# A fused two-block kernel on one Trainium2 core: the last unit of the gate z moves from the projection stage to the head of the delta stage

## The chip, the cores and the metric

The kernel runs on one core of a Trainium2 chip. The metric is the device time of one launch in microseconds (us). Everything below is in us unless a row says ns.

## What is computed

The reference runs a block of two layers (a mixer and a feed-forward part each) and then a second block. The change lies in the mixer of the first block, which runs once per layer, so twice in a launch. Cut to what matters here:

```python
p = h @ w_in                       # h: 512 tokens x 1024
(qkv, z, beta_r, a_r, hq, ...) = _split(p, IN_SIZES)
qkv = silu(_dwconv(qkv, dn_conv))  # q, k, v of 4 heads x 128; q and k are brought to unit norm
o_f = _gated_delta_rule(q, k, v, beta[0], g[0])
o_b = _flip(_gated_delta_rule(_flip(q), _flip(k), _flip(v), _flip(beta[1]), _flip(g[1])))
o_dn = o_f + o_b
o_dn = o_dn * rsqrt(mean(o_dn**2) + EPS) * dn_norm * silu(z)
```

z is 512 wide. It is made in four units of 128 rows, one for each head, and is needed only when the delta rule's output is gated, after the delta rule is done.

## The kernel before, in words

Everything is kept as 128-partition tiles of 512 columns (the tokens). A dense product of a weight tile and the input is made of three matmuls for each of eight k tiles, because weights and input are each split into a high part (rounded) and a low part (the rest): `product` (lines 142 to 148) writes high x high (L145), high x low (L146) and low x high (L147). One unit of 128 output rows is 24 matmuls of 512 columns. The queues of the five engines are written out by hand; each stage is one block, all engines leave a block together, and the engines meet by semaphores inside it.

The mixer's stages around the change:

- `qkv_stage` (line 332) makes 16 units: 12 for q, k and v and 4 for z (units 12 to 15). SP loads the raw weights of each unit into one of four buffers; ScalarE (ACT) rounds them (`high`, L379 to L383), GpSimd (POOL) or VectorE (DVE) makes the low part, TensorE (PE) multiplies (`dense`, L454 to L457). At the end of PE's queue stand unit 14, the transposes of the values (`turned_values`, L479 to L487) and then unit 15. At the end of ACT's queue stand the copies of the turned values (L440) and, in a loop over four, the SiLU of each z unit from its PSUM bank into Z (L441 to L443). The squares that the norms need lie in the buffer OHG during this stage.
- `delta_stage` (line 617) runs the delta rule in chunks of 128 tokens, in two directions (lanes 0 and 1, m counts the chunks). Its head, before the loop over m: PE makes the small gate sums (`gates_small`, L748, 16 columns each), the cumulated gates (`cumulated`, L758) and the products of keys with keys (`keys`, L766). DVE and ACT make decays from them (L1027, L925), DVE the masked scores (L1038), ACT scales them by beta (L939), POOL masks them for each level (`level_mask`, L676, tile LB). Then the triangular inverse is built level by level: `level_p` on PE (L786), a copy by ACT (`keep_p`, L952), `level_d` on PE (L794), a subtraction and a transpose by DVE (L1054, L1057). SP loads the next stage's first weights, 2 MB, at the start of this stage. The buffer OHG is free at first; the delta rule's R and VN lie in it from the first chunk's end on.
- `hgrn_proj_stage` (line 1153) makes the next products, and DVE multiplies the normed output of the delta stage by Z (L1327). ACT makes SiLUs there anyway (L1282).

The PSUM has eight banks; lane 0 of the delta stage has banks 0 to 3, lane 1 banks 4 to 7. Bank 2 of lane 0 is first written by `queries`, in turn m = 1 of the loop.

The lines that set the order at the seam are these (PE's queue at the end of `qkv_stage`, ACT's, and PE's head of `delta_stage`):

```python
                for h in range(4):
                    turned_values(h)
                dense(15)
...
                for j in range(4):
                    act.wait_ge(used, 13 + j)
                    act.activation(Z[:, j, :], PS[:, (12 + j) % 6, :], ACT.Silu).then_inc(S["z_done"], 1)
...
                for d in lanes:
                    keys(0, d)
                for m in range(CH + 1):
```

Of the kernel before, what the change touches and what calls it, by code (L numbers as in the profile page):

```python
# [14 lines left out]
P = 128  # L15
F32 = mybir.dt.float32
F32R = mybir.dt.float32r
# [313 lines left out]

def qkv_stage(nc, signals, PS, C, A, l, X, SS, XD, x_kept, pair, QKV, KTOK, VTOK, Z, BETA, G, SMALL, PAR, S1, S2, R, new):

# [13 lines left out]
    with signals.stage(*names) as sems:  # L347
# [12 lines left out]
        with nc.Block() as block:  # L360
# [17 lines left out]
            def _(act):  # L378
                def high(u):  # L379
                    act.wait_ge(loaded[u % N], 16 * (u // N + 1))  # L380
                    if u >= N:
                        act.wait_ge(used, u - N + 1)
                    act.copy(WHI[:, u % N], RAW[:, u % N]).then_inc(hi_s, 1)  # L383

# [53 lines left out]
                for h in range(4):  # L438
                    act.wait_ge(S["values_turned"], h + 1)
                    act.copy(tok(VTOK, h), PS[:, 6 + (h + 1) % 2, :].rearrange("p (c d) -> p c d", d=P)).then_inc(S["values_kept"], 1)  # L440
                for j in range(4):  # L441
                    act.wait_ge(used, 13 + j)
                    act.activation(Z[:, j, :], PS[:, (12 + j) % 6, :], ACT.Silu).then_inc(S["z_done"], 1)  # L443

            @block.tensor
            def _(pe):
# [78 lines left out]
                for h in range(4):  # L525
                    turned_values(h)
                dense(15)

# [77 lines left out]
            @block.gpsimd  # L606
            def _(pool):
                for u in range(N, T):
                    pool.wait_ge(hi_s, u + 1)
                    pool.tensor_tensor(WLO[:, u % N], RAW[:, u % N], WHI[:, u % N], ALU.subtract).then_inc(lo_pool, 1)  # L610

# [4 lines left out]

def delta_stage(nc, signals, PS, C, QKV, KTOK, VTOK, BETA, G, O, spare, parked, new, early):

# [11 lines left out]
    for d in lanes:  # L630
# [6 lines left out]
    kinds = ("small", "ngc", "ld", "mk", "gc", "m", "eg", "e", "kk", "at", "aq", "atb", "aqb", "lb", "tt0", "tc", "p", "pc", "dd", "t",  # L637
             "p6", "tcd", "d6", "ttf", "qk", "qkc", "qkm", "kg", "ks", "r", "vn", "vnc", "qg", "o", "oc", "oa", "kd", "st", "sd", "su")
    with signals.stage(*[f"delta_{n}{d}" for n in kinds for d in lanes]) as sems:
# [14 lines left out]
        with nc.Block() as block:  # L654
# [89 lines left out]
            def _(pe):  # L744
# [24 lines left out]
                def queries(m, d):  # L769
                    if m:  # L770
                        pe.wait_ge(S["oc" if m <= 2 else "oa"][d], m if m <= 2 else m - 2)
                    for h in H4:
                        last = pe.matmul(hb(d, 2, h), k_of(h, chunk(m, d)), q_of(h, chunk(m, d)), start=True, stop=True)
                    last.then_inc(S["qk"][d], 1)
# [92 lines left out]
                for d in lanes:  # L867
                    keys(0, d)
                for m in range(CH + 1):
                    j, levels, after = m - 1, m < CH, m + 1 < CH  # L870
# [47 lines left out]
            def _(act):  # L918
# [64 lines left out]
                for m in range(CH + 1):  # L983
                    j, levels, after = m - 1, m < CH, m + 1 < CH

                    def keep(n):
                        if levels:
                            for d in lanes:
                                keep_p(m, d, n)

                    keep(1)
                    if m:
                        for d in lanes:
                            keep_last(j, d)
                    keep(2)
                    if after:
# [156 lines left out]
def hgrn_proj_stage(nc, signals, PS, C, CR, l, A, SMALL, pair, O, Z, dn_norm, LF, KK, HI, HQ, HG, new, early):  # L1153
# [8 lines left out]
    with signals.stage("weights_hi", "weights_lo", "projected", "vector_steps", "scalar_steps", "logits_in", "reach_in", "tables_cast", "bound",  # L1162
# [3 lines left out]
        for g in range(5):  # L1166
            pnames += [f"unit{g}_0", f"unit{g}_1"] if g < 3 else [f"unit{g}_{m}" for m in range(4)]
        proj = Steps(proj_s, pnames)
        act_st = Steps(act_s, [f"{a}{g}_{c}" for g in range(2) for q in (0, 2) for a in ("e", "ln1", "lnb", "inv") for c in (q, q + 1)]
                       + [f"hi{c}" for c in range(4)] + [f"silu{g}_{m}" for g in (3, 4) for m in range(4)])  # L1170
        dve_st = Steps(dve_s, [n for g in range(2) for q in (0, 2) for n in [f"lbe{g}_{c}" for c in (q, q + 1)] + [f"{a}{g}_{c}" for c in (q, q + 1) for a in ("er", "kk", "lf")]]
# [11 lines left out]
        with nc.Block() as block:  # L1183
# [50 lines left out]
            def _(act):  # L1234
# [41 lines left out]
                for c in range(4):  # L1276
                    act_st.done(act.copy(HI[:, c, :], bank(2, c)), f"hi{c}")
                act.wait_ge(dve_st.sem, dve_st.place["lf1_3"])
                for g, dst in ((3, HQ), (4, HG)):
                    for m in range(4):  # L1280
# [6 lines left out]
            def _(dve):  # L1287
# [37 lines left out]
                for h in range(4):  # L1325
                    dve.wait_ge(norm_s, h + 1)
                    dve.tensor_tensor(O[:, h, :], O[:, h, :], Z[:, h, :], ALU.mult).then_inc(norm_s, 1)  # L1327
                for m in range(4):
# [1705 lines left out]
def mixer_layers(nc, signals, PS, C, A, X, XD, SS, PARS, SMALLS, new_in):  # L3034
    for l in range(A["w_in"].shape[0]):
        PAR, SMALL = PARS[:, 2 * l:2 * l + 2, :], SMALLS[:, l, :]
        w_in_l = A["w_in"][l].rearrange("(k p) n -> p k n", p=P)
        with ExitStack() as ffn, ExitStack() as mix:
            new = new_in(mix)
            pair = split_pair(new)  # L3040
            ODN, OHG = new("ODN", [P, 4, 512]), new("OHG", [P, 4, 512])
            with ExitStack() as zs:
                new_r = new_in(zs, "right")
# [3 lines left out]
                with ExitStack() as dn:  # L3047
# [5 lines left out]
                    BETA = new("BETA", [P, 4, 8])  # L3053
                    G = new("G", [P, 4, 8])
                    with ExitStack() as w:
                        R = hgrn_early.raw[:, :, :, :].rearrange("p s k n -> p (s k n)").rearrange("p (t n) -> p t n", n=512)
                        qkv_stage(nc, signals, PS, C, A, l, X, SS, XD, x_kept, pair, QKV, KTOK, VTOK, Z, BETA, G, SMALL, PAR[:, 0, :], OHG, ODN, R, new_in(w))
                    delta_stage(nc, signals, PS, C, QKV, KTOK, VTOK, BETA, G, ODN, OHG, X, new, hgrn_early)
                LF = new_in(mix)("LF", [P, 8, 512])
# [52 lines left out]
```

## Time and profile before

| | us |
|---|---|
| time, median of 3 runs | 2964.24 |
| lowest and highest | 2963.05, 2968.63 |
| the profiled execution's own time | 2960.97 |
| its span | 2959.2 |
| busy in the span: PE matmul | 2815.0 (95%) |
| PE weight load | 2319.2 (78%) |
| DVE, ACT, POOL | 1488.1 (50%), 1179.8 (40%), 972.9 (33%) |

The times are those of whole runs. The span is that of one profiled execution, from its first instruction to its last; its own time lies 1.8 us above the span. A row of the timeline gives the start of a group of like instructions, the time they cover, the engine, the line, the operation, and in brackets how long the engine had been idle and what ended that. A row of the windows gives, for a stretch, what each engine was busy, then the granted TensorE clock as a share of full speed (1.00 is 2.4 GHz, 0.50 is 1.2 GHz), the DMA engines' mean share and GB/s.

### The profile page before, as it was taken

What the parts mean: (1) busy time and instruction counts of PE and PEld (TensorE: products, weight loads), DVE (VectorE), ACT (ScalarE), POOL (GpSimd) and SP (SyncE); (2) the same over time, 40 slices, a digit from 0 to 9 for tenths busy, and PEclk for the clock granted to TensorE, in tenths of its full rate; (3) what the DMA queues carried; (4) which work ended last, traced back from release to release, by engine and by line L of the source; (5) the groups of instructions that cost most, each with busy time, mean ns of one, the idle gap of its engine ahead of it and who ended that gap; (6) DMA issues with size and microseconds to landing.
All of it is one profiled execution on the core that took longest, in us unless ns stands there. A gap on an engine that the chain in (4) does not pass through costs nothing. (4 is left out here: it accounts for less than half of the span.)

```text
span 2959.2 us, 42579 instructions
## 1 busy us (share of the span) xinstructions
PE 2815.0 (95%) x17694; PEld 2319.2 (78%) x17694; DVE 1488.1 (50%) x2068; ACT 1179.8 (40%) x1870; POOL 972.9 (33%) x513
## 2 busy tenths in 40 slices
PE   7988998999999989989989999999899999999999
PEld 5788976878888867889778788888677767788887
DVE  5565556437616455655564376265585552531120
ACT  4563655333313235527553333132334652342231
POOL 1263021014534413630210244444272323344433
PEclk8999999999999999999999999999899999999999
DMA  5101202333423241022023334232432213333322
GB/s 168 52 8 58 84 1 73 87 108 99 118 75 102 69 115 57 3 71 72 2 72 96 111 93 120 73 105 59 124 86 63 72 54 89 95 99 93 100 86 78
DMA packets 420512, 235.91 MB, mean 80 GB/s; under 512 B 24052, under 2 KB 416866, under 8 KB 419682
## 3 DMA queue, kind: packets, MB, share of 16 engines
q1 hardware_dynamic: 419442, 233.18, 27.4%
q8 instruction: 141, 2.31, 0.3%
q14 instruction: 49, 0.40, 0.0%
q10 hardware_dynamic: 880, 0.02, 0.0%
HBM read 226.88 MB, written 6.29 MB: 79 GB/s over the span
## 5 line engine op out<-in xcount | busy, mean ns | idle before, releaser
L2188 POOL TENSOR_TENSOR WLO<-RAW,WHI 128x1024 fp32r<-128x1024 f32 (+1 forms) x202 | 528.9, 2625 | 963.7 <-ACT WHI L2027 963.7
L145 PE MATMUL PS<-HHI,WHI 128*128 128x512 f32 x1920 | 757.9, 395 | 3.6 <-DVE WLO L2857 2.2
L147 PE MATMUL PS<-HHI,WLO 128*128 128x512 f32 x1920 | 750.2, 391 | 0.0
L146 PE MATMUL PS<-HLO,WHI 128*128 128x512 f32 x1920 | 750.0, 391 | 0.0
L145 PEld LDWEIGHTS PS<-HHI,WHI 128*128 128x128 f32 x1920 | 361.4, 188 | 89.7 <-issue 7.4
L2027 ACT CAST WHI<-RAW 128x1024 fp32r<-128x1024 f32 (+1 forms) x202 | 221.6, 1101 | 514.0 <-PE PS L147 499.2
L146 PEld LDWEIGHTS PS<-HLO,WHI 128*128 128x128 f32 x1920 | 361.5, 188 | 78.4 <-issue 2.7
L147 PEld LDWEIGHTS PS<-HHI,WLO 128*128 128x128 f32 x1920 | 361.1, 188 | 77.3
L2177 DVE TENSOR_TENSOR X<-X,PS 128x512 f32<-128x512 f32 x48 | 33.0, 688 | 334.1 <-PE PS L147 334.1
L2160 DVE SCALAR_TENSOR_TENSOR ACC<-GP,PARS,ACC 128x512 f32<-128x512 f32 x88 | 163.1, 1853 | 3.1
L145 PE MATMUL PS<-MHI,WHI 128*128 128x512 f32 x384 | 150.6, 392 | 9.3 <-DVE LHID L2121 4.2
L2919 POOL TENSOR_TENSOR WLO<-RAW,WHI 128x1280 fp32r<-128x1280 f32 x31 | 91.3, 2946 | 198.2 <-ACT WHI L2802 198.2
L147 PE MATMUL PS<-MHI,WLO 128*128 128x512 f32 x384 | 149.6, 390 | 0.0
L146 PE MATMUL PS<-MLO,WHI 128*128 128x512 f32 x384 | 149.5, 389 | 0.0
L145 PE MATMUL PS<-WHI,HHI 128*128 128x256 f32 x448 | 129.7, 290 | 10.9 <-DVE WLO L197 10.7
L193 ACT CAST WHI<-RAW 128x1536 fp32r<-128x1536 f32 (+1 forms) x52 | 85.2, 1641 | 124.7 <-PE PS L147 101.9
L146 PE MATMUL PS<-WLO,HHI 128*128 128x256 f32 x448 | 128.4, 287 | 0.0
L147 PE MATMUL PS<-WHI,HLO 128*128 128x256 f32 x448 | 128.4, 287 | 0.0
L197 DVE TENSOR_TENSOR WLO<-RAW,WHI 128x1536 fp32r<-128x1536 f32 (+1 forms) x52 | 101.9, 1960 | 50.4 <-ACT WHI L193 49.3
L610 POOL TENSOR_TENSOR WLO<-RAW,WHI 128x1024 fp32r<-128x1024 f32 x24 | 57.6, 2415 | 182.0 <-ACT WHI L383 182.0
L2639 POOL TENSOR_TENSOR WLO<-RAW,WHI 128x1024 fp32r<-128x1024 f32 x20 | 81.5, 4094 | 107.2 <-ACT WHI L2300 107.2
L2153 DVE TENSOR_TENSOR GP<-PS,RS 128x512 f32<-128x512 f32 x44 | 30.4, 692 | 152.8 <-PE PS L147 128.0
(481 smaller groups left out, 5224.5 us busy)
## 6 DMA issues: line engine op xcount, KB each, us to landing
RAW<-in_w_up SPq DMA_DIRECT2D x88, 512.0 KB, 3.8
RAW<-in_w_in SPq DMA_DIRECT2D x82, 512.0 KB, 4.1
RAW<-in_w_mlp SPq DMA_DIRECT2D x64, 512.0 KB, 3.9
RAW<-in_w_down SPq DMA_DIRECT2D x32, 704.0 KB, 4.5
RAW<-in_w_in SPq DMA_DIRECT2D x20, 1024.0 KB, 5.3
RAW<-in_w_gate SPq DMA_DIRECT2D x32, 512.0 KB, 3.7
RAW<-in_w_out SPq DMA_DIRECT2D x24, 512.0 KB, 4.9
x_kept<-X SPq DMA_DIRECT2D x2, 2048.0 KB, 9.4
```

Of the source, the lines that this page charges most:

```text
L145: e.matmul(out, wh, xh, start=first and n == 0, stop=False)
L146: e.matmul(out, wh, xl, start=False, stop=False)
L147: last = e.matmul(out, wl, xh, start=False, stop=final and n == len(quads) - 1)
L193: self.hi_st.done(act.copy(self.hi[:, s], self.raw[:, s]), f"unit{s}")
L197: self.lo_st.done(dve.tensor_tensor(self.lo[:, s], self.raw[:, s], self.hi[:, s], ALU.subtract), f"unit{s}")
L610: pool.tensor_tensor(WLO[:, u % N], RAW[:, u % N], WHI[:, u % N], ALU.subtract).then_inc(lo_pool, 1)
L2027: ac.done(act.copy(slot(WHI, u), source(u)), f"hi{u}")
L2160: dv.done(dve.scalar_tensor_tensor(acc, gp[:, n:n + 512], tap(n), acc, ALU.mult, ALU.add), f"tap{n}_{i}")
L2177: dv.done(dve.tensor_tensor(X[:, m, :], X[:, m, :], PS[:, 6 + m % 2, :], ALU.add), f"x{g}_{m}")
L2188: pool.tensor_tensor(slot(WLO, u), source(u), slot(WHI, u), ALU.subtract).then_inc(lo_s, 1)
L2639: pool.tensor_tensor(WLO[:, u % N], RAW[:, u % N], WHI[:, u % N], ALU.subtract).then_inc(S["lo_pool"], 1)
L2919: pool.tensor_tensor(WLO[:, u % 3], RAW[:, u % 3], WHI[:, u % 3], ALU.subtract).then_inc(lo_s, 1)
```

## The change

Unit 15, the last unit of z, is taken out of the projection stage on PE and ACT and made in the delta stage. Its weights are still loaded, rounded (ACT) and split (POOL) in `qkv_stage`, but into two tiles that lie in OHG (`late`), which the squares held. ACT's rounding of this unit no longer waits for a weight buffer to come free. PE makes the 24 matmuls in the delta stage behind the keys of chunk 0, into bank 2 of lane 0, from there ACT copies them to Z unscaled between the first and second level's copies, and the SiLU of this part of Z is made in place in `hgrn_proj_stage`. `queries` of lane 0 waits once for the copy, DVE's last multiplication with Z once for the SiLU. The DMA queue is the same.

```diff
                 def high(u):
                     act.wait_ge(loaded[u % N], 16 * (u // N + 1))
-                    if u >= N:
+                    if N <= u < T - 1:
                         act.wait_ge(used, u - N + 1)
-                    act.copy(WHI[:, u % N], RAW[:, u % N]).then_inc(hi_s, 1)
+                    act.copy(WHI[:, u % N] if u < T - 1 else late[0], RAW[:, u % N]).then_inc(hi_s, 1)
...
-                for j in range(4):
+                for j in range(3):
                     act.wait_ge(used, 13 + j)
                     act.activation(Z[:, j, :], PS[:, (12 + j) % 6, :], ACT.Silu).then_inc(S["z_done"], 1)
...
                 for h in range(4):
                     turned_values(h)
-                dense(15)
...
-                    pool.tensor_tensor(WLO[:, u % N], RAW[:, u % N], WHI[:, u % N], ALU.subtract).then_inc(lo_pool, 1)
+                    pool.tensor_tensor(WLO[:, u % N] if u < T - 1 else late[1], RAW[:, u % N], WHI[:, u % N] if u < T - 1 else late[0], ALU.subtract).then_inc(lo_pool, 1)
...
                 def queries(m, d):
                     if m:
                         pe.wait_ge(S["oc" if m <= 2 else "oa"][d], m if m <= 2 else m - 2)
+                    elif d == 0:
+                        pe.wait_ge(S["zc"][0], 1)
...
                 for d in lanes:
                     keys(0, d)
+                product(pe, bank(0, 2), [(late[0][:, k, :], late[1][:, k, :], pair[0][:, k, :], pair[1][:, k, :]) for k in range(8)]).then_inc(S["z"][0], 1)
                 for m in range(CH + 1):
...
                     if m:
                         for d in lanes:
                             keep_last(j, d)
+                    else:
+                        act.wait_ge(S["z"][0], 1)
+                        act.copy(Z[:, 3, :], bank(0, 2)).then_inc(S["zc"][0], 1)
                     keep(2)
...
                 act.wait_ge(dve_st.sem, dve_st.place["lf1_3"])
+                act_st.done(act.activation(Z[:, 3, :], Z[:, 3, :], ACT.Silu), "siluz")
                 for g, dst in ((3, HQ), (4, HG)):
...
                 for h in range(4):
                     dve.wait_ge(norm_s, h + 1)
+                    if h == 3:
+                        dve.wait_ge(act_st.sem, act_st.place["siluz"])
                     dve.tensor_tensor(O[:, h, :], O[:, h, :], Z[:, h, :], ALU.mult).then_inc(norm_s, 1)
...
+            ohg_at = nc._sbuf_addr_for_side("left") - 4 * 4 * 512
...
+                    late = [nc.alloc_sbuf_tensor_at(f"ZW{part}_{l}", [P, 8, P], F32R, offset=ohg_at + 4096 * part)[:, :, :] for part in range(2)]
```

PE's order before, from the turned values (L486) over the last rows of unit 15 (L145 to L147; HHI and HLO are the input, WHI and WLO the weights) to the delta stage's first rows, gates (L748) and cumulated gates (L758):

```order
363 L486 MATMUL PS<-C,QKV 128x128 x16
364 L145 MATMUL PS<-HHI,WHI 128x512
365 L146 MATMUL PS<-HLO,WHI 128x512
366 L147 MATMUL PS<-HHI,WLO 128x512
...
388 L360 UNCONDITIONAL_BRANCH
389 L743 UNCONDITIONAL_BRANCH
390 L748 MATMUL PS<-G,C 128x16 x3
391 L758 MATMUL PS<-C,G 128x128 x4
```

PE's order with the change, from the same place to the first level's products (L787, which was L786):

```order
363 L486 MATMUL PS<-C,QKV 128x128 x16
364 L360 UNCONDITIONAL_BRANCH
365 L742 UNCONDITIONAL_BRANCH
366 L747 MATMUL PS<-G,C 128x16 x3
367 L757 MATMUL PS<-C,G 128x128 x4
368 L747 MATMUL PS<-G,C 128x16 x3
369 L757 MATMUL PS<-C,G 128x128 x4
370 L765 MATMUL PS<-QKV 128x128 x8
371 L145 MATMUL PS<-HHI,ZW_0_226 128x512
...
394 L147 MATMUL PS<-HHI,ZW_0_227 128x512
395 L787 MATMUL PS<-T_1,LB_1 64x64 x16
```

The 24 matmuls of the unit have left their place ahead of the branch and stand between the keys and the first level.

ACT's order with the change, from the copies of the values (L440) to the levels' copies (L954, which was L952):

```order
74 L440 COPY VTOK<-PS 128x4x128 x4
75 L443 ACTIVATE Z<-PS 128x512 x3
76 L360 UNCONDITIONAL_BRANCH
77 L919 UNCONDITIONAL_BRANCH
78 L977 ACT_TABLE_LOAD
...
86 L954 COPY PP_1<-PS 128x256 x2
87 L999 COPY Z<-PS 128x512
88 L954 COPY PP_1<-PS 128x256 x2
```

Three SiLUs stand ahead of the branch where there were four, and the copy of Z is new between two pairs of the levels' copies, which stood together as four.

## Rows read from the trace of the kernel before

**Rows 1.** The page, busy time, share of the span and instructions of each engine.
```profile
PE 2815.0 (95%) x17694; PEld 2319.2 (78%) x17694; DVE 1488.1 (50%) x2068; ACT 1179.8 (40%) x1870; POOL 972.9 (33%) x513
```
**Rows 2.** Timeline, PE, end of the projection stage, first layer (start, us covered).
```profile
134.04 1.12 PE L486 MATMUL PS<-C,QKV 128*128 128x128 f32 x8 [0.33 <-ACT VTOK L440]
134.92 0.47 PE L145 MATMUL PS<-HHI,WHI 128*128 128x512 f32 x1
...
140.24 0.39 PE L147 MATMUL PS<-HHI,WLO 128*128 128x512 f32 x1
```
**Rows 3.** Timeline, ACT, end of the projection stage, first layer, then second layer.
```profile
135.68 1.58 ACT L443 ACTIVATE Z<-PS 128x512 f32<-128x512 f32 x3
140.66 0.60 ACT L443 ACTIVATE Z<-PS 128x512 f32<-128x512 f32 x1 [3.40 <-PE PS L147]
...
1167.73 1.58 ACT L443 ACTIVATE Z<-PS 128x512 f32<-128x512 f32 x3
1172.72 0.60 ACT L443 ACTIVATE Z<-PS 128x512 f32<-128x512 f32 x1 [3.40 <-PE PS L147]
```
**Rows 4.** Timeline, PE, head of the delta stage, first layer.
```profile
141.57 0.81 PE L748 MATMUL PS<-G,C 128*128 128x16 f32 x6 [0.94 <-PEq L360]
...
145.69 2.65 PE L766 MATMUL PS<-QKV 128*128 128x128 f32 x16
152.27 1.99 PE L786 MATMUL PS<-T,LB 64*64 64x64 f32 x32 [3.93 <-POOL LB L676]
154.06 1.92 PE L794 MATMUL PS<-PP,TT 64*64 64x64 f32 x32
155.76 1.86 PE L786 MATMUL PS<-T,LB 64*64 64x64 f32 x32
157.55 2.05 PE L758 MATMUL PS<-C,G 128*128 128x128 f32 x16
```
**Rows 5.** Timeline, PE, head of the delta stage, second layer.
```profile
1173.62 0.81 PE L748 MATMUL PS<-G,C 128*128 128x16 f32 x6 [0.94 <-PEq L360]
...
1176.94 2.05 PE L766 MATMUL PS<-QKV 128*128 128x128 f32 x16
1182.95 1.99 PE L786 MATMUL PS<-T,LB 64*64 64x64 f32 x32 [3.96 <-POOL LB L676]
...
1188.30 2.05 PE L758 MATMUL PS<-C,G 128*128 128x128 f32 x16
```
**Rows 6.** Windows over both heads: each engine's busy time, then PEclk, DMA share, GB/s.
```profile
142.00:144.00 2.00, 2.00 (x19) 2.00 (x19) 0.26 (x2) 1.07 (x3) 1.94 (x6) 0.94 0.62 137
146.00:148.00 2.00, 2.00 (x15) 2.00 (x15) 1.06 (x3) 1.49 (x5) 0.00 (x0) 0.71 1.10 348
150.00:152.00 2.00, 0.00 (x0) 0.00 (x0) 1.30 (x3) 1.98 (x10) 1.50 (x3) 0.64 0.00 0
156.00:158.00 2.00, 2.00 (x36) 1.93 (x34) 0.89 (x3) 0.71 (x2) 1.02 (x2) 0.65 0.00 0
1180.00:1182.00 2.00, 0.00 (x0) 0.00 (x0) 1.46 (x4) 1.98 (x9) 1.23 (x2) 0.85 0.61 192
1188.00:1190.00 2.00, 2.00 (x23) 1.90 (x20) 0.51 (x1) 0.37 (x1) 1.07 (x2) 0.94 0.00 0
```
**Rows 7.** Timeline, PE, levels at the full clock, same chunk, first layer.
```profile
165.63 1.15 PE L786 MATMUL PS<-T,LB 64*64 64x64 f32 x32
166.79 1.15 PE L794 MATMUL PS<-PP,TT 64*64 64x64 f32 x32
168.08 1.47 PE L786 MATMUL PS<-T,LB 64*64 64x64 f32 x32
169.42 0.68 PE L794 MATMUL PS<-PP,TT 64*64 64x64 f32 x16
```
**Rows 8.** Timeline, ACT, the levels' copies between which Z's copy comes, second layer.
```profile
1184.99 0.37 ACT L952 COPY PP<-PS 128x256 f32<-128x256 f32 x1 [0.50 <-PE PS L786]
1187.57 0.37 ACT L952 COPY PP<-PS 128x256 f32<-128x256 f32 x1 [2.20 <-PE PS L786]
```
**Rows 9.** Timeline, ACT, next projection stage, where the new SiLU comes.
```profile
350.30 2.04 ACT L1277 COPY HI<-PS 128x512 f32<-128x512 f32 x4
353.94 1.28 ACT L1282 ACT_TABLE_LOAD   x1 [1.60 <-PE PS L147]
```

More of the change, by code:

```diff
@@ L329, in tile, with qkv_stage @@
     return buf[:, k, :] if isinstance(k, int) else buf[:, ds(k, 1), :].rearrange("p a n -> p (a n)")
-def qkv_stage(nc, signals, PS, C, A, l, X, SS, XD, x_kept, pair, QKV, KTOK, VTOK, Z, BETA, G, SMALL, PAR, S1, S2, R, new):
+def qkv_stage(nc, signals, PS, C, A, l, X, SS, XD, x_kept, pair, QKV, KTOK, VTOK, Z, BETA, G, SMALL, PAR, S1, S2, R, late, new):
     K, N, T = 8, 4, 16
@@ L609, in _, with delta_stage @@
                     pool.wait_ge(hi_s, u + 1)
-                    pool.tensor_tensor(WLO[:, u % N], RAW[:, u % N], WHI[:, u % N], ALU.subtract).then_inc(lo_pool, 1)
+                    pool.tensor_tensor(WLO[:, u % N] if u < T - 1 else late[1], RAW[:, u % N], WHI[:, u % N] if u < T - 1 else late[0], ALU.subtract).then_inc(lo_pool, 1)
 def per_head(bank):
     return bank.rearrange("p (h n) -> p h n", h=4)
-def delta_stage(nc, signals, PS, C, QKV, KTOK, VTOK, BETA, G, O, spare, parked, new, early):
+def delta_stage(nc, signals, PS, C, QKV, KTOK, VTOK, BETA, G, O, spare, parked, late, pair, Z, new, early):
     lanes = (0, 1)
@@ L637, in delta_stage @@
     kinds = ("small", "ngc", "ld", "mk", "gc", "m", "eg", "e", "kk", "at", "aq", "atb", "aqb", "lb", "tt0", "tc", "p", "pc", "dd", "t",
-             "p6", "tcd", "d6", "ttf", "qk", "qkc", "qkm", "kg", "ks", "r", "vn", "vnc", "qg", "o", "oc", "oa", "kd", "st", "sd", "su")
+             "p6", "tcd", "d6", "ttf", "qk", "qkc", "qkm", "kg", "ks", "r", "vn", "vnc", "qg", "o", "oc", "oa", "kd", "st", "sd", "su", "z", "zc")
     with signals.stage(*[f"delta_{n}{d}" for n in kinds for d in lanes]) as sems:
@@ L1169, in hgrn_proj_stage @@
         act_st = Steps(act_s, [f"{a}{g}_{c}" for g in range(2) for q in (0, 2) for a in ("e", "ln1", "lnb", "inv") for c in (q, q + 1)]
-                       + [f"hi{c}" for c in range(4)] + [f"silu{g}_{m}" for g in (3, 4) for m in range(4)])
+                       + [f"hi{c}" for c in range(4)] + ["siluz"] + [f"silu{g}_{m}" for g in (3, 4) for m in range(4)])
         dve_st = Steps(dve_s, [n for g in range(2) for q in (0, 2) for n in [f"lbe{g}_{c}" for c in (q, q + 1)] + [f"{a}{g}_{c}" for c in (q, q + 1) for a in ("er", "kk", "lf")]]
@@ L3054, in mixer_layers @@
                     G = new("G", [P, 4, 8])
+                    late = [nc.alloc_sbuf_tensor_at(f"ZW{part}_{l}", [P, 8, P], F32R, offset=ohg_at + 4096 * part)[:, :, :] for part in range(2)]
                     with ExitStack() as w:
                         R = hgrn_early.raw[:, :, :, :].rearrange("p s k n -> p (s k n)").rearrange("p (t n) -> p t n", n=512)
-                        qkv_stage(nc, signals, PS, C, A, l, X, SS, XD, x_kept, pair, QKV, KTOK, VTOK, Z, BETA, G, SMALL, PAR[:, 0, :], OHG, ODN, R, new_in(w))
-                    delta_stage(nc, signals, PS, C, QKV, KTOK, VTOK, BETA, G, ODN, OHG, X, new, hgrn_early)
+                        qkv_stage(nc, signals, PS, C, A, l, X, SS, XD, x_kept, pair, QKV, KTOK, VTOK, Z, BETA, G, SMALL, PAR[:, 0, :], OHG, ODN, R, late, new_in(w))
+                    delta_stage(nc, signals, PS, C, QKV, KTOK, VTOK, BETA, G, ODN, OHG, X, late, pair, Z, new, hgrn_early)
                 LF = new_in(mix)("LF", [P, 8, 512])
```

## The prediction, on record before the changed kernel was run

> **What bounds the kernel now.** I read the page's busy times first. PE is busy 95% of the span and no other engine over 50% [rows 1], so the kernel can gain only where PE stands idle or runs at its low clock, and the sum has to be made at such a place. The change touches one such place in each of two layers: the seam between the projection stage and the delta stage. So the timelines of PE and ACT across the seam came next, then the windows for the clock. What the reader is to see in them: at the end of the projection stage PE is dense (a matmul each 0.23 us), then ACT has one SiLU to make, for which it had waited 3.40 us [rows 3], and PE starts again 0.31 us after that SiLU's end (140.66 + 0.60 = 141.26 against 141.57 [rows 3, 4]). In the delta stage's head PE does some 7 us of work and then stands idle for 3.93 us in the first layer and 3.96 us in the second, until POOL has made the first level's masks [rows 4, 5]. That hole is long enough for most of a z unit.
>
> **What the change moves, part by part.** The sum is made against the profiled execution's own time, 2960.97 us (its span is 2959.2); the median of the three runs is 2964.24, 3.3 us above it, and the forecast is the sum added to the median. Per seam:
>
> (a) *The stage ends earlier.* Unit 15 on PE goes from 134.92 to the start of its last matmul at 140.24 [rows 2], 23 steps of 0.231 us, so 24 x 0.231 = 5.55 us. The stage does not get shorter by that. ACT still has the three other SiLUs, which lay beside unit 15 and now stand open: they end at 135.68 + 1.58 = 137.26, where the stage ended at 141.26. In the second layer it is 1167.73 + 1.58 = 1169.31 against 1172.72 + 0.60 = 1173.32 [rows 3]. That is -4.0 us each, -8.0 us in both. The cover of 1.6 us that unit 15 gave to ACT is the cost of this edit.
>
> (b) *The unit in the hole.* It starts when the keys are done. From there to the first level was 3.93 and 3.96 us [rows 4, 5]; the unit takes 5.55 us at the full clock. So the first level starts 1.6 us later: +3.2 us in both.
>
> (c) *The clock in the head.* In the first layer the clock stood at its low level (1.2 GHz) from about 143.8 to 147.2: the windows show 0.94 of full speed over 142 to 144 and 0.71 over 146 to 148 [rows 6]. (At half speed for a share f of a window its row shows 1 - f/2; 0.94 is 0.24 us low at the window's end, 0.71 is 1.16 us low at its start.) Ahead of the fall PE had stood idle for 0.94 us and then done light work, the gates' six matmuls of 16 columns; ahead of the rise it had worked without a gap. In the second layer it did not fall there. The price of that short stretch is the difference of the two heads: 152.27 - 141.57 = 10.70 us against 1182.95 - 1173.62 = 9.33 us [rows 4, 5], so 1.4 us. With the change PE's idle time ahead of the stage grows from 0.94 us to 2.4 us (137.57 less 134.04 + 1.12 = 135.16, the end of the turned values [rows 2]), followed by the same light work. I therefore expect a fall in both layers. Whether it is a short stretch, or one twice as long, is open: the later low stretches of this trace, where PE stood idle for some time after the fall as well, lasted from 150.6 to 157.4 and from 1181.4 to 1188.2 [rows 6], about twice as long as the first. A long stretch is priced at twice the short one, 2.8 us. I take one short and one long: 1.4 + 2.8 - 1.4 (already paid) = +2.8 us. The ends are no fall at all (-1.4 us) and two long ones (+4.2 us).
>
> The Trainium skill (TensorE: Matmul & The Clock Gate, HAM oscillation — how this bites in real kernels) speaks against this change: idle time between bursts of matmuls throws the array back to the low clock, so that the next burst starts cold. By that rule the sum would hold both heads wholly cold, the upper end of (c). The same page (Part 1: The HAM clock gate) says that the moments of change are not tied to the program and differ from run to run; the two layers here, alike in work and unlike in clock, agree.
>
> (d) *The clock in the levels.* The hole was the cause of the second fall: the first three steps (level, its second product, level) ran at half speed, from 152.27 to 157.55, 5.28 us, and from 1182.95 to 1188.30, 5.35 us [rows 4, 5]. At the full clock the same steps take 166.79 - 165.63 = 1.16, 168.08 - 166.79 = 1.29 and 169.42 - 168.08 = 1.34 us [rows 7], 3.8 us together. Behind 24 dense matmuls the clock should be high: -1.5 us each, -3.0 us in both. The ends are 0 (something other than PE sets these steps) and -3.4 us (1.15 for the last step).
>
> (e) *Costs taken as nothing, with their cover.* ACT's copy of Z, about 0.6 us like the SiLU of the same tile, falls between two copies that had 1187.57 - 1184.99 - 0.37 = 2.2 us of idle time between them [rows 8]; at the full clock some 1.5 us of it are left, and it still fits. Were the cover gone, the second level would be late by up to 0.6 us. The keys' queries that wait for it come a whole turn later. The new SiLU in the next stage takes the place between the HI copies' end at 352.34 and the table load at 353.94, which it pulls ahead; there are 1.6 us of idle time and then a table load of 1.28 us [rows 9] that no longer waits for the product, so PE, dense there, sees nothing. ACT's rounding of unit 15 loses a wait that it did not stand in. POOL and SP issue what they did before; the 2 MB for the next stage start 4 us earlier and nobody waits for them. In the second layer the keys kept 0.128 us per matmul (2.05 / 16 [rows 5]) while those bytes came in, so the unit is not slowed by them.
>
> Sum: -8.0 + 3.2 + 2.8 - 3.0 = **-5.0 us**, so 2956.0 beside the profiled execution and **2959.2 us** as a median. With the ends: -8.0 + 3.2 - 1.4 - 3.4 = -9.6 us and -8.0 + 3.2 + 4.2 - 0 = -0.6 us, so 2954.6 to 2963.6.
>
> **The rivals.**
> 1. *The clock stays high in both heads.* For it: the second layer's head held the full clock. Against it: the idle time in front more than doubles. Then (c) is -1.4: -8.0 + 3.2 - 1.4 - 3.0 = -9.2 us, 2955.0 us.
> 2. *The levels don't get shorter.* Between two products stand an ACT copy, a DVE subtraction and POOL's masks. If these set the pace in the first three steps, (d) is 0: -2.0 us, 2962.2 us. Against it: rows 7 have the same chain.
> 3. *The stage doesn't open earlier*, because what opens the delta stage is not ACT's last SiLU. The 0.31 us between them is the same in both layers, which speaks against it. Then (a) is 0: +3.0 us, 2967.2 us.
> 4. *Slower: the clock stays low through the unit.* The unit stands behind the long idle time and the light work; if the clock does not rise until the unit is over, its 24 matmuls cost 11.1 us instead of 5.55. The place is PE between keys and first level, the price +5.55 us in each layer on top of both heads cold: -8.0 + 3.2 + 4.2 - 3.0 + 11.1 = +7.5 us, 2971.7 us. It decides against the change from 1.8 us more per unit (7.4 us), and to over 0.2% from 4.75 us more (10.3 us). Against it: in the first layer the clock rose at 147.2, while the keys, dense like the unit, were running. The Trainium skill (TensorE: Matmul & The Clock Gate, Back-to-back issue gap) gives columns / 1.2 GHz for a cold matmul, an estimate of 24 x 0.427 = 10.2 us for the unit by that page; with it the rival would be at +5.8 us.
>
> **How the numbers follow.** A measurement of this kernel can tell about 0.2%, 5.9 us, from no change, so faster by that means 2958.3 or less. The forecast's case, with one to two long stretches or none, has 0.62; it goes from -3.6 us (both long) over -5.0 to -6.4 us (both short), and with the scatter of runs I put 0.21 of it beyond -5.9. Rival 1 has 0.13, all faster. Rival 2 has 0.15, all within. Rival 3 has 0.05, within. Rival 4 has 0.05, slower. Faster 0.34, same 0.61, slower 0.05. The range of 2954 to 2964 takes in the ends of the unknown terms and rivals 1 and 2, and leaves out rivals 3 and 4.
>
> **What would show it.** Right: the delta stage's first gates start 0.3 us after the third SiLU of Z, 4.0 us earlier relative to the values' copies; the unit's matmuls follow the keys with no wait and 0.23 us apart; the first level follows the unit with no idle time; the granted clock is low before or in the keys and 1.00 from the unit to the next cumulated gates; those come 3.8 us after the first level. Wrong: a granted clock of 0.50 during the unit, an idle time of PE between unit and first level, levels still over 5 us apart at the full clock, or an ACT wait for the unit that delays the second level's copy.

## The result, and the profile after

| | kernel before | changed kernel |
|---|---|---|
| median of 20 runs each | 2964.99 | 2973.43 |
| lowest and highest | 2962.15, 2968.82 | 2956.07, 2978.43 |
| the profiled execution's own time, its span | 2960.97, 2959.2 | 2963.89, 2962.1 |

The ratio is 1.0021, with a 95% interval of 1.0011 to 1.0031: slower by 0.2%, where the forecast was 2959.2 us, 5 us faster. (The ratio lies nearer to that of the means, 2971.4 to 2965.4 us, than to that of the medians, because the changed kernel's runs are unevenly spread over 22 us.) That spread, against 7 us before, is the second finding: in this series the changed kernel's fastest run is 6 us faster than any of the kernel before, and its slowest 10 us slower. The 7 us are the narrowest case: in four later series of 15 to 29 runs the kernel before itself spread over 13 to 16 us (2957.28 to 2974.74 in all), its median staying at 2963.8 to 2965.1.

The page of the changed kernel, busy times. They answer to [rows 1]; PE is busy 9.4 us longer with the same 17694 instructions:

```profile
PE 2824.4 (95%) x17694; PEld 2327.7 (79%) x17694; DVE 1488.4 (50%) x2068; ACT 1180.8 (40%) x1872; POOL 972.5 (33%) x513
```

Timeline of ACT at the end of the projection stage, first layer, then second (start, us covered); they answer to [rows 3]:

```profile
134.40 1.58 ACT L443 ACTIVATE Z<-PS 128x512 f32<-128x512 f32 x3
136.25 1.28 ACT L977 ACT_TABLE_LOAD   x1 [0.27 <-PEq L360]
...
1162.12 1.58 ACT L443 ACTIVATE Z<-PS 128x512 f32<-128x512 f32 x3
1163.97 1.28 ACT L977 ACT_TABLE_LOAD   x1 [0.27 <-PEq L360]
```

Timeline of PE in the delta stage's head, first layer; it answers to [rows 4]:

```profile
136.29 0.81 PE L747 MATMUL PS<-G,C 128*128 128x16 f32 x6 [2.41 <-PEq L360]
...
140.50 2.57 PE L765 MATMUL PS<-QKV 128*128 128x128 f32 x16
148.48 1.15 PE L787 MATMUL PS<-T,LB 64*64 64x64 f32 x32
149.63 1.15 PE L795 MATMUL PS<-PP,TT 64*64 64x64 f32 x32
150.93 1.47 PE L787 MATMUL PS<-T,LB 64*64 64x64 f32 x32
152.33 2.05 PE L757 MATMUL PS<-C,G 128*128 128x128 f32 x16
```

and second layer, answering to [rows 5]:

```profile
1164.01 0.81 PE L747 MATMUL PS<-G,C 128*128 128x16 f32 x6 [2.41 <-PEq L360]
...
1168.49 3.62 PE L765 MATMUL PS<-QKV 128*128 128x128 f32 x16
1177.78 1.15 PE L787 MATMUL PS<-T,LB 64*64 64x64 f32 x32
...
1181.63 2.05 PE L757 MATMUL PS<-C,G 128*128 128x128 f32 x16
```

In this profiled run the seam did what was forecast. The stage opens 0.31 us after the third SiLU's end (134.40 + 1.58 = 135.98, then 136.29); PE's idle time ahead of it is 2.41 us; the hole is filled, with no idle time in front of the first level; and the three steps of the levels take 152.33 - 148.48 = 3.85 us where they took 5.28. The windows show the clock as in term (c), a short stretch in the first layer and a long one in the second. It is high again before the unit in the first layer and 0.8 us into the unit in the second (its first two matmuls begin 0.57 and 0.36 us apart, the others 0.23). The windows answer to [rows 6]:

```profile
138.00:142.00 4.00, 4.00 (x23) 4.00 (x23) 1.54 (x4) 2.07 (x8) 1.39 (x4) 0.57 1.08 364
142.00:148.00 6.00, 6.00 (x33) 5.11 (x32) 4.62 (x10) 4.88 (x19) 3.21 (x5) 1.00 0.29 90
1166.00:1172.00 6.00, 6.00 (x29) 6.00 (x30) 2.80 (x7) 3.40 (x13) 1.10 (x4) 0.50 0.97 320
```

Where the time went shows when the same rows of ACT's timeline are set side by side through the launch:

| place | before | changed | difference |
|---|---|---|---|
| first of the three SiLUs of Z, layer 1 | 135.68 | 134.40 | -1.3 |
| first rounding behind the delta stage, layer 1 | 268.31 | 263.08 | -5.2 |
| start of the hgrn stage, layer 1 | 392.86 | 387.55 | -5.3 |
| start of the branch stage, layer 1 | 503.98 | 498.60 | -5.4 |
| first of the three SiLUs of Z, layer 2 | 1167.73 | 1162.12 | -5.6 |
| first rounding behind the delta stage, layer 2 | 1299.10 | 1292.46 | -6.6 |
| start of the hgrn stage, layer 2 | 1423.64 | 1417.55 | -6.1 |
| start of the branch stage, layer 2 | 1534.75 | 1532.99 | -1.8 |
| end of the span | 2959.2 | 2962.1 | +2.9 |

The seams gained 3.9 us in the first layer and 1.0 us in the second, 5.0 us together, the forecast's own figure; that it is so exact is luck, since this run drew the one short and one long stretch that the forecast had taken, and other runs drew longer ones. Then 4.3 us went in the second layer's hgrn stage, to which the change did nothing, and 4.7 us behind it. Windows over that stage in the changed kernel:

```profile
1435.00:1439.00 4.00, 3.65 (x41) 3.53 (x42) 4.00 (x13) 0.59 (x1) 0.02 (x1) 0.57 0.00 0
1462.00:1466.00 4.00, 4.00 (x32) 3.29 (x28) 4.00 (x13) 1.65 (x3) 0.00 (x0) 0.59 0.02 4
1490.00:1494.00 4.00, 3.92 (x28) 3.48 (x28) 4.00 (x13) 1.34 (x3) 0.00 (x0) 0.57 0.01 4
```

and over the same places in the kernel before (6 us later):

```profile
1439.00:1443.00 4.00, 1.71 (x40) 1.38 (x37) 4.00 (x8) 0.00 (x0) 2.11 (x2) 1.00 0.00 0
1467.00:1471.00 4.00, 4.00 (x62) 3.35 (x59) 4.00 (x13) 2.07 (x4) 0.00 (x0) 1.00 0.02 4
1495.00:1499.00 4.00, 4.00 (x48) 2.92 (x48) 4.00 (x13) 2.88 (x7) 0.00 (x0) 1.00 0.02 4
```

Three new stretches at 0.50 (the mean over 4 us is 0.57 to 0.59), where the kernel before holds 1.00. Each begins in or up to 1.3 us behind a pause that PE makes once in a chunk for DVE: 2.29 and 2.23 us in the first two chunks of the layer, and in two parts of 1.33 and 1.06 us in the third. In the fourth chunk the parts are 0.65 us each and no stretch follows. The first of them in the timeline:

```profile
1430.98 2.09 PE L1472 MATMUL PS<-hX 128*64 128x64 f32 x64
1435.36 1.94 PE L1472 MATMUL PS<-hX 128*64 128x64 f32 x32 [2.29 <-DVE hX L1616]
```

The kernel before has the same pause and keeps its clock:

```profile
1441.44 1.36 PE L1464 MATMUL PS<-hX 128*64 128x64 f32 x32 [2.29 <-DVE hX L1608]
```

So the question was what makes the clock fall in one and not in the other. **Theory A:** the moments at which the chip decides on the clock are its own; the pause is harmless where it stands well against them, and the change has moved the stage. **Theory B:** the loss is a property of the seam, its longer idle time and low stretches.

### The profile page after: what moved, and what is told of

Its sections match the earlier page's. It is cut to its first block and busy times, and to the rows that moved or that the text cites. A ratio compares the mean times of both kernels' runs of the same rounds, so it can differ in the third digit from the quotient of the medians.

```text
span 2962.1 us, 42576 instructions
## 1 busy us (share of the span) xinstructions
PE 2824.4 (95%) x17694; PEld 2327.7 (79%) x17694; DVE 1488.4 (50%) x2068; ACT 1180.8 (40%) x1872; POOL 972.5 (33%) x513
## 5 line engine op out<-in xcount | busy, mean ns | idle before, releaser
L145 PE MATMUL PS<-HHI,WHI 128*128 128x512 f32 x1904 | 752.5, 395 | 3.6 <-DVE WLO L2865 2.2
L147 PE MATMUL PS<-HHI,WLO 128*128 128x512 f32 x1904 | 744.9, 391 | 0.0
L145 PEld LDWEIGHTS PS<-HHI,WHI 128*128 128x128 f32 x1904 | 358.8, 188 | 88.9 <-issue 7.7
L147 PEld LDWEIGHTS PS<-HHI,WLO 128*128 128x128 f32 x1904 | 358.6, 188 | 76.6
L145 PE MATMUL PS<-MHI,WHI 128*128 128x512 f32 x384 | 150.8, 393 | 9.7 <-DVE LHID L2129 4.2
L147 PE MATMUL PS<-MHI,WLO 128*128 128x512 f32 x384 | 149.8, 390 | 0.0
L145 PE MATMUL PS<-WHI,HHI 128*128 128x256 f32 x448 | 130.1, 290 | 10.8 <-DVE WLO L197 10.7
L147 PE MATMUL PS<-WHI,HLO 128*128 128x256 f32 x448 | 128.8, 288 | 0.0
```

Source lines behind the costliest of these rows:

```text
L145: e.matmul(out, wh, xh, start=first and n == 0, stop=False)
L147: last = e.matmul(out, wl, xh, start=False, stop=final and n == len(quads) - 1)
```

## The experiments

**1 and 2. The kernel before, shifted.** In both layers ScalarE gets 2 (then 4) copies of a scratch tile at the end of the stage ahead of the hgrn stage. Nothing else changes, and the output is the same.

```diff
                         if g == 3 and m % 2:
                             feed.split_hi(act, 4, m // 2)
+                for k in range(2):
+                    act.wait_ge(root_s, 8 + k)
+                    act.copy(SQ[:, 0, :], SQ[:, 1, :]).then_inc(root_s, 1)
```

> The kernel before, with two small ScalarE copies added behind the last SiLU of the stage ahead of the hgrn stage, in each layer; they hold that stage's start back by about 1.3 us and touch nothing else. Theory A (the clock falls in the hgrn stage where that stage's once-a-chunk pause of TensorE meets the moments at which the chip looks, and the change only moved the stage against those moments): the hgrn stage of both layers shows falls or none depending on the shift, by the same number of chunks in both layers; time 2964.99 + 2.6 = 2967.6 us without falls, some 1.4 us more per fall, up to 8 falls, so up to 2979. Theory B (the loss of the change comes from the seam itself, its longer stretches at the low clock): no fall in the hgrn stage, 2967.6 us, with runs as close together as those of the kernel before (within 7 us).

> The kernel before, with four such copies, about 2.7 us per layer. Theory A: this puts the hgrn stage of both layers where the changed kernel's second layer stood (0.76 of the distance between two such moments behind one, where the kernel before stood at 0.97 to 1.0), so falls of the granted clock in about three chunks of each layer, 6 x 1.4 us over the shift's own 5.4 us: about 2964.99 + 5.4 + 8.4 = 2979 us. Theory B: 2964.99 + 5.4 = 2970.4 us and no fall in the hgrn stage.

Measured: 2974.75 us with two copies (2972.83 to 2976.47, 5 runs) and 2972.17 us with four, against 2964.82 us of the kernel before in the same session; ratios 1.0038 (1.0026 to 1.0051) and 1.0032 (1.0020 to 1.0045). Two copies of 0.6 us in each layer cost 10 us. Windows over the hgrn stages of the kernel before with two copies, first layer, then second:

```profile
411.00:415.00 4.00, 3.67 (x41) 3.56 (x42) 4.00 (x13) 0.59 (x1) 0.00 (x0) 0.57 0.00 0
438.00:442.00 4.00, 4.00 (x32) 3.25 (x28) 4.00 (x13) 1.68 (x3) 0.00 (x0) 0.60 0.00 0
466.00:470.00 4.00, 3.93 (x28) 3.52 (x28) 4.00 (x13) 1.32 (x3) 0.00 (x0) 0.57 0.00 0
1453.00:1457.00 4.00, 4.00 (x34) 3.39 (x34) 3.73 (x12) 1.74 (x4) 0.00 (x0) 0.63 0.00 0
1480.00:1484.00 4.00, 4.00 (x42) 3.16 (x41) 3.10 (x10) 2.37 (x4) 0.00 (x0) 0.59 0.00 0
1507.00:1511.00 4.00, 4.00 (x28) 3.33 (x27) 3.82 (x12) 1.61 (x3) 0.00 (x0) 0.57 0.00 0
```

The very pattern of the changed kernel, now in both layers, in a kernel whose seam is untouched. This is what theory B excludes. The hgrn stage took 116.5 and 116.8 us (from ACT's first rounding in it to the first of the next stage), where it takes 111.1 in both layers of the kernel before; a further fall stood at its start in each. The copies also lengthen PE's idle time ahead of the stage, from 0.94 to 2.10 us, so those two falls may come from that and not from where the stage stands. With four copies my expectation missed: 2979 us by theory A, and the 2972.17 measured lie nearer to theory B's 2970.4. Of the three pauses per layer one met a fall, and a stretch of 6.8 us came at the stage's start in both layers, behind 3.40 us of idle time, for 114.8 and 113.1 us. That a shift can bring falls is shown; my map of which shift does what was wrong.

**3 and 4. The pause filled.** In each chunk of the hgrn stage TensorE gets seven matmuls of 256 columns in the pause, whose result nobody reads.

```diff
+                def keep_warm(m, count):
+                    pe.wait_ge(S["ac"][1], m * (LEVELS - 1) + 2)
+                    for k in range(count):
+                        pe.matmul(acc(1, 1)[:, 256:512], C[:, IDENT, :], C[:, 0:2, :].rearrange("p a n -> p (a n)"), start=True, stop=True)
...
+                        if n == 2:
+                            keep_warm(m, 7)
                         if n == 0:
                             exponents(m, 1, 1)
```

> The changed kernel, with seven extra matmuls of 256 columns (their result is never read) in each chunk of the hgrn stage, where TensorE pauses for 2.3 us, into the unused half of a PSUM bank. Theory A: no fall in the hgrn stage of either layer in any run, the runs come together (within some 8 us instead of 22), and the median falls from 2973.43 by the 10 to 15 us that the falls cost, to 2958 to 2963 us. Theory B: the median stays at about 2973 us and the runs stay 22 us apart.

> The kernel before with the same extra matmuls, the control. Both theories: within 2 us of the kernel before (2963 to 2967 us), since its hgrn stages showed no fall; a loss of more would mean that the extra matmuls themselves cost time.

Measured: the changed kernel 2961.78 us (2957.58 to 2964.18, 11 runs; ratio 0.9991, 0.9981 to 1.0000), the kernel before with the same matmuls 2964.99 us (2958.21 to 2967.79, 11 runs; ratio 1.0005, 0.9996 to 1.0014); the kernel before alone 2964.82 us. As theory A has it, the changed kernel's runs lie within 7 us, no fall is left in the pauses of the profiled run, and the change, beside its partner with the same matmuls, is now worth 3.2 us (by the means 3.5, with a 95% interval of 1.2 to 5.8). The changed kernel without the matmuls did not run in this series; in two later ones it spread over 11 and 18 us around 2965 to 2966 us, so the 12 us down from 2973.43 are not all shown to be the matmuls' gain. The filled pause in the changed kernel, timeline of PE:

```profile
402.72 3.29 PE L1478 MATMUL PS<-C 128*128 128x256 f32 x14
405.94 1.15 PE L1472 MATMUL PS<-hX 128*64 128x64 f32 x32
```

It also shows that seven are too many: 3.29 us in a pause of 2.3 us. In the profiled run of the kernel before with these matmuls the hgrn stages took 114.2 and 113.1 us instead of 111.1, 5 us more in all, though its median did not rise; where that came back was not looked for.

**5 and 11. The changed kernel again**, unaltered.

> The changed kernel once more, for another profile of it, since its runs lie between 2956 and 2978 us. Theory A: where the profiled run is above 2970 us, the stretches at the low clock that are new against the kernel before lie in the hgrn stages, one in each of three or four chunks, 27.3 us apart, in both layers; the seam between projection and delta stage differs by no more than one stretch (3.4 us low, 1.4 us of time) per layer. Theory B: the extra low time lies in the seam and the stage behind it.

> The changed kernel a third time, for more times: 20 runs gave a median of 2973.43 us and 8 later ones 2965.23 us. Theory A: the runs are a mixture, by how the stages come to stand against the moments at which the chip looks, of some near 2960 us (no fall in the hgrn stages), some near 2965 to 2970 (one layer) and some near 2977 (both), so the spread is again over 12 us and the median lies between 2963 and 2976 us. Theory B (a fixed cost of the change) expects one value within some 6 us.

Measured: 2965.23 us (2963.74 to 2974.34, 8 runs; ratio 1.0002, 0.9989 to 1.0014) and 2966.00 us (2959.66 to 2977.98, 11 runs; ratio 1.0010, 0.9997 to 1.0023). So the loss of the first series is not a constant of the kernel, and in the later two series no loss is clear of noise: over all 39 runs the median is 2967.8 us, that of 106 runs of the kernel before 2964.7 us. The profiled run of 2974.34 us had one fall at the start and one behind a pause of the first layer's hgrn stage and three in the second's, and longer stretches in both heads of the delta stage than I had thought of. The profiled run of the third series, 2961.18 us, missed the expectation that a run near 2960 us has no fall there: it had two in the pauses of the first layer's hgrn stage (114.4 us instead of 111.1) and none in those of the second's, and 6.8 us at the low clock in each head. Its windows over the two falls:

```profile
435.00:439.00 4.00, 4.00 (x31) 3.09 (x28) 3.42 (x11) 2.18 (x4) 0.00 (x0) 0.57 0.02 4
462.00:466.00 4.00, 3.57 (x27) 3.26 (x28) 4.00 (x14) 1.17 (x2) 0.00 (x0) 0.58 0.00 0
```

So falls in this stage and the time of the whole launch don't go together run by run; other stages differ between runs too. Timeline and windows of the first layer's head in the run of 2974.34 us:

```profile
137.76 1.43 PE L747 MATMUL PS<-G,C 128*128 128x16 f32 x6 [2.41 <-PEq L360]
...
143.87 3.55 PE L765 MATMUL PS<-QKV 128*128 128x128 f32 x16
...
152.81 1.15 PE L787 MATMUL PS<-T,LB 64*64 64x64 f32 x32
```

```profile
137.00:141.00 4.00, 3.24 (x16) 3.27 (x16) 0.26 (x2) 2.00 (x4) 2.81 (x8) 0.50 0.52 138
141.00:145.00 4.00, 4.00 (x21) 4.00 (x21) 1.54 (x4) 1.70 (x7) 0.00 (x0) 0.50 1.10 362
145.00:149.00 4.00, 4.00 (x20) 3.70 (x20) 2.69 (x7) 2.77 (x11) 0.74 (x1) 0.72 0.09 28
```

Here the clock fell in the idle time ahead of the stage and stayed low for 10.2 us, up to the unit. Both theories had a share in this run: A in the hgrn stages, B in the heads.

**6. Four matmuls instead of seven**, in the changed kernel.

> The changed kernel with four extra matmuls per chunk of the hgrn stage instead of seven. The seven took 3.29 us where the pause was 2.30 us and put the next level 0.6 us later in each of eight chunks. Theory A: four take 1.9 us, fit in the pause and still keep the clock high: no falls in the hgrn stage, and about 4 us less than the 2961.78 us with seven, so 2957 to 2959 us. If four are too few, falls come back in some runs and the median lies above 2962 us with a spread over 10 us. Theory B has no reason for a difference beyond the 4 us.

Measured: 2958.16 us (2954.21 to 2961.25, 12 runs), ratio 0.9974 (0.9964 to 0.9984), and the spread is again 7 us. The time is as expected. The expectation of no fall in the hgrn stage was missed in the profiled run: none is in a pause, but one lies near the first layer's stage start, ahead of the first pause:

```profile
397.00:401.00 4.00, 3.88 (x11) 3.08 (x12) 0.83 (x3) 3.05 (x6) 2.57 (x3) 0.62 0.00 0
```

**7 and 12. The seam kept warm.** On top of that, nine matmuls of 512 columns behind the turned values, in the 2.4 us that TensorE waits for ScalarE.

```diff
                 for h in range(4):
                     turned_values(h)
+                pe.wait_ge(S["taps"], 60)
+                for _ in range(9):
+                    pe.matmul(PS[:, 5, :], pair[0][:, 0, 0:P], pair[0][:, 0, :], start=True, stop=True)
```

> As the run before, and nine extra matmuls of 512 columns on TensorE behind the turned values, in the 2.4 us in which it waits for ScalarE's three SiLUs of Z. This takes away the cause that the forecast named for term (c). If (c) is right, the clock no longer falls in the delta stage's head in either layer, the keys take 2.05 us instead of 2.6 to 3.6 us, and the kernel is 1.4 us to 5.6 us faster than the run before, likeliest 3 to 4: about 2954 us. If the light work of the gates alone makes the clock fall, nothing changes there and the times are within 1 us of each other.

> The fastest version again (changed kernel, four extra matmuls per chunk of the hgrn stage, nine at the seam), which had 6 runs with a median of 2950.73 us. Theory A: no fall in either delta stage's head and none in the pauses of the hgrn stage, so 2948 to 2953 us, and faster than the kernel before by 0.4 to 0.6%. Theory B has no reason for it to be below 2956 us, the change's forecast.

Measured: 2950.73 us (2943.54 to 2956.72, 6 runs; ratio 0.9947, 0.9928 to 0.9966) and 2944.16 us (2942.76 to 2950.40, 5 runs; ratio 0.9936, 0.9923 to 0.9948). Timeline of PE in the first layer's head, and windows over the heads of both layers, in the first of the two:

```profile
135.05 2.30 PE L529 MATMUL PS<-HHI 128*128 128x512 f32 x9
137.74 0.81 PE L750 MATMUL PS<-G,C 128*128 128x16 f32 x6 [0.39 <-PEq L360]
...
141.06 2.05 PE L768 MATMUL PS<-QKV 128*128 128x128 f32 x16
148.52 1.15 PE L790 MATMUL PS<-T,LB 64*64 64x64 f32 x32
```

```profile
137.00:142.00 5.00, 4.61 (x38) 4.14 (x37) 1.80 (x6) 3.15 (x10) 2.81 (x8) 1.00 0.64 195
1166.00:1170.00 4.00, 3.87 (x33) 3.75 (x34) 1.58 (x6) 2.37 (x7) 2.81 (x8) 1.00 0.70 204
```

No fall in either head, in this profiled run and in that of the second series. From the first gates to the first level it is now 148.52 - 137.74 = 10.78 us, in the second layer 10.77. This version beats the kernel before by 14.4 and 20.5 us and the unfilled changed kernel of the same two series by 14.5 and 21.8 us. The second series was faster than I had expected (2948 at the lowest), and the terms do not add up to all of it: the low stretches that went elsewhere in the launch were not taken apart.

**8. The shifted kernel with the pause filled.**

> The kernel before with the two ScalarE copies that made it 9.9 us slower (2974.75 us), and with the seven extra matmuls per chunk of the hgrn stage. Theory A: the same shift costs only itself: no falls in the hgrn stage, about 2.6 us over the 2964.99 us of the kernel before with these matmuls, 2967.6 us. Theory B, or any cost of the copies themselves: it stays near 2975 us.

Measured: 2967.68 us (2964.83 to 2973.41, 10 runs; ratio 1.0010, 0.9998 to 1.0022), against 2974.75 without the matmuls. Windows over the same three places of the first layer as in experiment 1:

```profile
411.00:415.00 4.00, 4.00 (x50) 3.38 (x50) 4.00 (x12) 0.80 (x2) 0.24 (x1) 1.00 0.00 0
438.00:442.00 4.00, 4.00 (x76) 3.43 (x76) 3.87 (x12) 2.06 (x4) 0.00 (x0) 1.00 0.02 4
466.00:470.00 4.00, 4.00 (x49) 3.31 (x50) 4.00 (x13) 2.27 (x5) 0.00 (x0) 1.00 0.02 6
```

Filling the pause takes away 7 of the 10 us. What is left holds the shift's own cost and, against the expectation, a fall at the start of the hgrn stage in both layers (the windows 395 to 399 and 1429 to 1433 us have a granted clock of 0.57).

**9 and 10. The partner with four matmuls, and term (d) alone.** The second of them also has 16 matmuls of 512 columns in the delta stage's hole, the unit staying where it was.

```diff
                 for d in lanes:
                     keys(0, d)
+                for _ in range(16):
+                    pe.matmul(bank(0, 2), HH[:, 0, 0:P], HH[:, 0, :], start=True, stop=True)
```

> The kernel before with four extra matmuls per chunk of the hgrn stage, the partner of the run of the changed kernel with the same four (2958.16 us). Theory A with the forecast's terms (a) to (d): the change is worth 3 to 5 us between these two, so this one lies at 2961 to 2963 us, and with no fall in the hgrn stage's pauses. If the whole gain over the kernel before came from the extra matmuls, it lies at 2958 us too.

> As the run before, with 16 extra matmuls of 512 columns (3.6 us, their result is never read) in the hole of the delta stage's head, in the place where the change puts the unit of z, and the unit left where it was. This is term (d) alone: the clock stays high behind the hole, the first three steps of the levels take 3.8 us instead of 5.3 us in each layer, and the time is 3.0 us less than in the run before. If something else than the clock sets these steps, they stay at 5.3 us and the time does not move.

Measured: 2962.67 us (2951.66 to 2964.38, 11 runs; ratio 0.9989, 0.9978 to 1.0000) and 2959.08 us (2954.32 to 2961.03, 11 runs; ratio 0.9981, 0.9972 to 0.9989). By the medians the change is worth 2962.67 - 2958.16 = 4.5 us where the pause is filled with four matmuls. The partner has two runs near 2952 us, though, one of them the profiled one, and ran in another series: by the means it is 2.7 us, with a 95% interval of 3.0 either way, so the size is not sure. Warming the hole alone is worth 3.6 us by the medians and 1.9, again with 3.0 either way, by the means. The traces show 1.7 us of it: the three steps took 153.71 - 149.68 = 4.03 us in the first layer and 4.02 in the second, where the run before had 4.86 and 4.91, not 5.3. That the hole's idle time set the clock of the steps is shown, the -3.0 us are not:

```profile
145.46 3.90 PE L870 MATMUL PS<-HHI 128*128 128x512 f32 x16
149.68 0.68 PE L786 MATMUL PS<-T,LB 64*64 64x64 f32 x16 [0.32 <-POOL LB L676]
150.55 0.68 PE L786 MATMUL PS<-T,LB 64*64 64x64 f32 x16 [0.19 <-POOL LB L676]
...
153.71 2.05 PE L758 MATMUL PS<-C,G 128*128 128x128 f32 x16
```

## Why the prediction was wrong

The step that failed first is the frame of the sum. "The change touches one such place in each of two layers", I wrote, and the forecast added up the two seams and nothing else. The seams came out as added in the profiled run, -5.0 us. What the sum lacked, a term that stood in it at nothing, is that a stage to which nothing was done can cost more when it begins at another moment: 4.3 us in the profiled run's second layer. The second step that failed is the size of term (c): +5.5 us where the sum had +2.8, from all profiled runs together. I had read the rule that bears on the first of them, and used it for the head of the delta stage alone: the Trainium skill (TensorE: Matmul & The Clock Gate, Part 1: The HAM clock gate) says that the chip's moments are not tied to the program and differ from run to run. The traces agree: the unaltered changed kernel had its falls in the pauses of the hgrn stages as none and three (first and second layer), one and three, and two and none in its three profiled runs. I did not ask which other stages hold a pause that would turn into a fall, and rows with DVE as the releaser of PE in the hgrn stage were there to be found. None of the four rivals named it either. Point by point:

- **(a)** right: -4.0 us each, with 0.31 us between the third SiLU and the gates. Rival 3 is out.
- **(b)** 10.78 us from gates to first level with the clock high (experiment 7) against 9.33: +1.45 us each, forecast 1.6.
- **(c)** the mechanism was right, the size too small. From gates to first level the changed kernel and its variants with an idle seam took 12.2, 13.8, 12.2, 13.8, 15.1, 15.2, 15.5, 12.2, 13.8 and 13.8 us, on average 13.7, so 3.0 us per head over 10.78; the kernel before and its variants with the head as it was took 9.33 in ten of twelve heads and 10.70 in two, so 0.2 us. Term (c) is therefore +2.7 us per layer, +5.5 us in all where I had +2.8, and beyond my upper end of 4.2; experiment 7, with the idle time filled and no fall, shows that the cause is the one named. I had taken the kernel before to pay for a fall in every second head, from one trace, and two lengths of stretch for the only ones; there was a third, of 10.2 us, worth 4.3 to 4.7.
- **(d)** the mechanism was right: 3.85 us in every head of the changed kernel, forecast 3.8. The kernel before had 4.86 to 5.36 over its variants, so the gain was 1.0 to 1.5 us, on average 1.2 where I had 1.5. Rival 2 is out.
- **(e)** right: ACT's copy of Z had ended 1.1 us before the next copy was due, and the new SiLU in the next stage with its table load (347.05 and 348.35) held nobody up: the first HQ SiLU follows it at 348.89, where the old order, 5.3 us earlier, would have had it at 355.24 - 5.30 = 349.94.
- **Rival 4**, the clock low through the unit, was not seen: in the profiled runs the clock rose before the unit or at most 0.9 us into it. In the prediction I had the rule of the Trainium skill on idle time between bursts (TensorE: Matmul & The Clock Gate, HAM oscillation — how this bites in real kernels) ask for both heads wholly cold. That was misread: the page speaks of longer idle times than the 2.41 us of this seam, and by it alone no fall was due. The measurement decides: all ten heads of the changed kernel and its variants with the idle seam had a fall.

By these sizes the sum is -8.0 + 2.9 + 5.5 - 2.5 = -2.1 us for the seams, and with the pauses filled the pairs gave -3.2 and, less surely, -4.5 us. What takes that away in the kernel as it is, is in part the falls in the hgrn stages: 4.3 us in the first profiled run, some 6 us in that of experiment 5 and 3.3 us in that of experiment 11. Open: how the 14 us between forecast and median of the first series divide beyond that, why the 20 runs of the first series lay higher than the 19 later ones, which shifts meet a fall (my map failed in experiment 2), and the 4.7 us that the profiled run lost behind the mixer, where new stretches also show but no experiment was made.

## What to carry to other kernels

Where the span holds pauses of TensorE like those here (1 to 2.4 us, with light matmuls beside them), list them all before costing a change of a few us: each is a possible fall of the clock, and a shift of what lies ahead can decide which of them pays. A difference of 0.2% between two such kernels says little on the edit itself; compare them with the pauses filled, over ten runs or more. Cheap matmuls in a pause, no longer than it, were worth more here than the change: 4 in each chunk and 9 at the seam took 14.5 and 21.8 us off the changed kernel.

## What was not expected of the hardware

Two ScalarE copies of 0.6 us per layer, behind which nothing waits but the next stage, cost 10 us. The falls in the pauses of the hgrn stages come in up to three chunks in a row, 27.3 us apart (1435.4, 1462.7 and 1490.1 us in the changed kernel), while the pauses follow each other at nearly the same distance (they end at 1435.36, 1461.40 and 1490.09). So one bad stand is paid up to three times per layer, some 1.4 us each (4.3 us for three). And the time of a run of one and the same kernel ranged over 22 us with its mean granted clock: 0.983 at 2956.07 us and 0.974 at 2978.43 us, with one run out of line (0.981 at 2971.32 us).
